# A three-layer transformer kernel on one core: TensorE multiplies constants into the next accumulator before late operands

## What is computed

```
for i in range(DEPTH):                       # DEPTH = 2
    h = rms_norm(x, norm_mix[i]) * (1.0 + sc1) + sh1
    y = mla_mixer(h, ...) if i % 2 == 0 else gdn_mixer(h, ...)
    x = x + g1 * y
    h = rms_norm(x, norm_ffn[i]) * (1.0 + sc2) + sh2
    y = swiglu_ffn(h, ...) if i % 2 == 0 else moe_ffn(h, ...)
    x = x + g2 * y
x = rms_norm(x, final_norm)
x = x + rms_norm_2(merged @ w_out[l], norm_mix_post[l])   # merged: the four gated branches
f = (silu(h @ ffn_w_gate[l]) * (h @ ffn_w_up[l])) @ ffn_w_down[l]
x = x + rms_norm_2(f, norm_ffn_post[l])
```

## Time and profile before

| | |
|---|---|
| median of three runs | 3055.1 us (3048.0 to 3055.36) |
| the profiled execution | 3062.7 us, its span 3061.4 us |
| TensorE busy | 2843.2 us, 93% of the span |
| VectorE busy | 1717.6 us, 56% |
| ScalarE busy | 1235.7 us, 40% |
| GpSimd busy | 248.7 us, 8% |
| mean granted TensorE clock | 0.965 |
| DMA, mean over the span | 127 GB/s |

### The profile page before, as it was taken

How to read it: one execution, slowest core, us unless ns; L and a number is a source line. 1 busy time by engine, 2 the same in 40 slices (tenths; PEclk the granted TensorE clock), 3 DMA queues, 4 the chain that set the end, 5 groups by cost and what they waited for, 6 DMA issues and landing times. The chain is left out here.

```text
span 3061.4 us, 36282 instructions
## 1 busy us (share of the span) xinstructions
PE 2843.2 (93%) x14489; PEld 2326.9 (76%) x14489; DVE 1717.6 (56%) x2889; ACT 1235.7 (40%) x2128; POOL 248.7 (8%) x224
## 2 busy tenths in 40 slices
PE   5988899999997989989999997999999999899998
PEld 4766687877886879778877775788788766678886
DVE  6666455444873857444468886543425386654344
ACT  2455432223433343333467775432223345432222
POOL 0000000000002543010000001112100002200000
PEclk8889999999999999989999999999999999999999
DMA  5222234332222111064579995211231203412321
GB/s 221 76 109 102 83 144 172 137 128 93 96 110 90 56 42 56 1 222 140 186 269 367 342 362 208 76 66 42 101 113 46 83 31 129 150 69 81 116 83 66
DMA packets 72096, 387.66 MB, mean 127 GB/s; under 512 B 8234, under 2 KB 9934, under 8 KB 36174
## 3 DMA queue, kind: packets, MB, share of 16 engines
q1 hardware_dynamic: 58512, 349.20, 31.4%
q10 hardware_dynamic: 10382, 26.07, 2.4%
q0 software_dynamic: 3024, 9.98, 0.9%
HBM read 368.43 MB, written 22.03 MB: 128 GB/s over the span
## 5 line engine op out<-in xcount | busy, mean ns | idle before, releaser
L343 DVE TENSOR_TENSOR wlo<-stage,whi 128x1024 fp32r<-128x1024 f32 (+3 forms) x504 | 531.5, 1095 | 356.2 <-ACT whi L355 354.8
L355 ACT ACTIVATE whi<-stage 128x1024 fp32r<-128x1024 f32 (+3 forms) x504 | 440.4, 922 | 230.8 <-PE ps L639 195.8
L639 PE MATMUL ps<-bxhi,whi 128*128 128x512 f32 x480 | 200.9, 418 | 17.1 <-DVE bxlo L343 8.4
L639 PE MATMUL ps<-whi,mxhi 128*128 128x512 f32 (+1 forms) x528 | 204.2, 387 | 9.9 <-DVE wlo L343 7.8
L639 PE MATMUL ps<-whi,mxlo 128*128 128x512 f32 (+1 forms) x528 | 197.8, 375 | 0.0
L639 PE MATMUL ps<-wlo,mxhi 128*128 128x512 f32 (+1 forms) x528 | 197.5, 374 | 0.0
L639 PE MATMUL ps<-bxhi,wlo 128*128 128x512 f32 x480 | 190.4, 397 | 0.0
L639 PE MATMUL ps<-bxlo,whi 128*128 128x512 f32 x480 | 189.9, 396 | 0.0
L343 DVE TENSOR_TENSOR wlo<-more,whi 128x1024 fp32r<-128x1024 f32 (+1 forms) x126 | 142.2, 1171 | 44.3 <-ACT whi L355 43.1
L351 DVE SCALAR_TENSOR_TENSOR part<-stage,small,part 128x256 f32<-128x256 f32 x273 | 157.9, 579 | 9.7
L639 PE MATMUL ps<-gwide 128*128 128x128 f32 x1088 | 135.8, 285 | 13.4 <-POOL gwide L343 11.5
(11 more groups left out here) (591 smaller groups left out, 6311.6 us busy)
## 6 DMA issues: line engine op xcount, KB each, us to landing
stage<-in_gu SPq DMA_DIRECT2D x92, 1024.0 KB, 5.5
stage<-in_ada SPq DMA_DIRECT2D x40, 1024.0 KB, 5.1
more<-in_gu SPq DMA_DIRECT2D x40, 1024.0 KB, 7.0
stage<-in_dn SPq DMA_DIRECT2D x26, 768.0 KB, 4.5
stage<-in_dn SPq DMA_DIRECT2D x19, 1024.0 KB, 7.1
stage<-in_gin SPq DMA_DIRECT2D x16, 1024.0 KB, 4.9
stage<-in_gt SPq DMA_DIRECT2D x16, 1024.0 KB, 5.0
more<-in_dn SPq DMA_DIRECT2D x13, 1024.0 KB, 6.7
```

The costliest lines, as they stand in the source:

```text
L343: return e.do.tensor_tensor(out, x, y, op)
L355: return e.do.activation(out, x, f, **kw)
L639: return self.p.do.matmul(out, lhsT, rhs, start=start, stop=stop, skip_group_check=True)
```

## The change

A new helper `pe_busy(ps, n)` issues n matmul calls of the block of ones by the first 512 columns of the constants, into the accumulator bank `ps` that the next real operation will overwrite. It stands behind the wait for the bank and ahead of the wait for the operands. Where a wait named operand and bank together, it is cut in two. By the diff there are fourteen places in the order of TensorE: wo 6, xs2 3, gu0 7, xs3 4, gin 7, gq of head 0 4, tt of heads 0, 1 and 4 with 7, 4 and 6, came 0, 1 and 2 with 6, 7 and 2, rw 16, gu2 9. This is 88 calls in one execution. (The part behind the branch is written once for each side of it, and one side runs.)

```diff
+    def pe_busy(self, ps, n):
+        for _ in range(n):
+            self.mm(ps[:, :], self.c("ones"), self.cst_all[:, 0:512])
...
                 if q == 0:
                     p.wait_ge(*vacant)
+                    if step == 0 and first == ids[0:lead]:
+                        self.pe_busy(ps, busy)
                 p.wait_ge(wt(kk), *ok(q))
...
-        self.p.wait_ge(mark, *vacant)
+        self.p.wait_ge(*vacant)
+        self.pe_busy(ps, busy)
+        self.p.wait_ge(mark)
...
-        for _ in self.pe_gemm("wo", "wo", range(4), L.X, lambda q: [V(("ot", "l", q))]):
+        for _ in self.pe_gemm("wo", "wo", range(4), L.X, lambda q: [V(("ot", "l", q))], busy=6):
...
-                for b, _ in enumerate(self.pe_gemm(k, k, ids, L.X, self.normed(L.n.key), lead=2)):
+                for b, _ in enumerate(self.pe_gemm(k, k, ids, L.X, self.normed(L.n.key), lead=2, busy=0 if e or len(ids) == 1 else 9 if layer else 7)):
...
-        self.pe_total("xs2", self.sq, self.V(("wo", "t", 6)), more=self.last_square)
+        self.pe_total("xs2", self.sq, self.V(("wo", "t", 6)), more=self.last_square, busy=3)
...
-        self.pe_total("xs3", self.sq, self.V(("f0", "t", 6)), more=self.last_square)
-        for k, _ in enumerate(self.pe_gemm("gin", "gin", range(16), L.X, self.normed("n3"), lead=2)):
+        self.pe_total("xs3", self.sq, self.V(("f0", "t", 6)), more=self.last_square, busy=4)
+        for k, _ in enumerate(self.pe_gemm("gin", "gin", range(16), L.X, self.normed("n3"), lead=2, busy=7)):
...
-                    self.pe_total(("gq", h), A1, A(("gq", h)))
+                    self.pe_total(("gq", h), A1, A(("gq", h)), busy=0 if h else 4)
...
-                    p.wait_ge(G(("tt", h)), *vac)
+                    p.wait_ge(*vac)
+                    self.pe_busy(b, {0: 7, 1: 4, 4: 6}.get(h, 0))
+                    p.wait_ge(G(("tt", h)))
...
-        p.wait_ge(V(("pick", n)), *vacant)
+        p.wait_ge(*vacant)
+        self.pe_busy(ps, (6, 7, 2, 0)[n])
+        p.wait_ge(V(("pick", n)))
...
-        for _ in self.pe_gemm("rw", "rw", range(4), L.X, L.ok, lead=2):
+        for _ in self.pe_gemm("rw", "rw", range(4), L.X, L.ok, lead=2, busy=16):
```

More of the change, by code:

```diff
@@ L582, in halved, with pe_gemm @@
         return hi, lo, lambda kk: self.V(("lo", i, int(kk >= (kc + 1) // 2)))
-    def pe_gemm(self, key, name, ids, X, ok, at=(None, None), lead=1):
+    def pe_busy(self, ps, n):
+        for _ in range(n):
+            self.mm(ps[:, :], self.c("ones"), self.cst_all[:, 0:512])
+    def pe_gemm(self, key, name, ids, X, ok, at=(None, None), lead=1, busy=0):
         p = self.p
@@ L725, in act_rstd, with pe_total @@
         act(a, dst, dst, ACT.Exp, scale=-0.5, **kw).then_inc(*A.up(event))
-    def pe_total(self, use, src, mark, ones=None, more=None):
+    def pe_total(self, use, src, mark, ones=None, more=None, busy=0):
         ps, vacant = self.take(use)
         ones = self.c("ones") if ones is None else ones
-        self.p.wait_ge(mark, *vacant)
+        self.p.wait_ge(*vacant)
+        self.pe_busy(ps, busy)
+        self.p.wait_ge(mark)
         z = self.mm(ps[:, :], ones, src, True, more is None)
```

## The result

The changed kernel took 3074.8 us (3073.3 to 3076.9, four runs) against 3053.2 us (3048.0 to 3055.4, four runs) for the kernel before: a ratio of 1.0073, with a 95% interval of 1.0057 to 1.0090. That is 22.3 us more (17 to 28), so slower by over 0.3%, as forecast; the forecast was +13.7 us on the median.

What follows compares the result with a forecast made beforehand. TensorE, busy 2843 of 3061 us, was taken to bound the kernel. Lateness less clock given back summed over the places to +13.7 us, 3068.8 us on the median of 3055.1; range 3052 to 3079 for 8 in 10.

Steps and rivals of the forecast that it cites:

- Rival 1: All places: fillers fit their room at 0.43 us a call, clock gives back 15.8 us, 3039 us; chance 0.08.
- Rival 3: All places: fillers don't hold the clock, 31 us of lateness paid without return, 3086 us; chance 0.07.
- Wo: At wo: filler 5.2 us in 3.76 of room, late 1.4, clock gives back 2.9; net -1.5 us.
- Route: At came 0, 1, 2: late 4 to 6 us, back 2.9; net +1.0 to +3.2, taken as +3.1 us.
- Rw: At rw: filler 13.8 us in 8.58 of room, late 5.2, back 2.3; net +2.9 us.
- Gu2: At gu2: filler 7.7 us in 5.16 of room, late 2.6, back 2.1; net +0.5 us.
- xs2 and gu0: First SwiGLU's sum and product: late 0.7 and 2.1 more, clock gives back 1.6; net +1.2 us.
- xs3 and gin: The next pair: late 1.8 and 2.1, clock gives back about 1.7; net +2.2 us.
- gq: Head 0's sums of squares: four fillers, clock back sooner than before; +2.3 us, bounds 0.7 and 4.1.
- tt of heads 0 and 1: Transposes of these heads: late 1.9 with 0.5 back, and no low clock; net +1.4 and +1.1 us.
- behind them up to 1280: tt of head 4: late 1.8 us, clock gives back 1.3; net +0.5 us.
- the two unknown prices: Uncertain costs at gq (0.7 to 4.1 us) and came (1.0 to 6), making the total +10 to +18.

Runs made afterwards that it cites:

- e8_rw_double: The changed kernel with 32 filler calls ahead of rw instead of 16: 3088.4 us, ratio 1.0118 to the kernel before.
- e6_came_only: The changed kernel with only the routing's fillers (came 6/7/2), all other counts 0: 3054.5 us, ratio 1.0012 to the kernel before.
- e5_gdn_only: The changed kernel with only the delta-net fillers (gq 4, tt 7/4/6), all other counts 0: 3064.2 us, ratio 1.0039 to the kernel before.

## Why the prediction was right in sign and short in size

**Right.** TensorE bounds the kernel, so a delay is paid in full: +22 for the whole, +13.5 for 13.7 us of fillers added (e8_rw_double). A call costs 0.86 us (13.90 us for 32 records). The waits are of length zero in front of the real operations, and the clock is 1.00 behind wo, gu0, gin, rw and gu2. Its mean rose from 0.965 to 0.974, where 0.98 was expected. The fillers of came 1 stand behind the branch; two of them ran at half clock in two of the three profiles that have them, none in e6_came_only. The parts add up: 6.1 (dense) + 11.9 (delta-net) + 3.7 (route) = 21.7, and the whole is 22.3 by its ratio. Rival 1 failed at its price. Fillers of that price are the half-width ones: they made the kernel faster, as it says, but by 7.6 us (4.9 to 10.4) and not by its 15.8. It had counted 2.9 us at the first expert product, where TensorE idles in the branch whatever the fillers cost. The Trainium skill, "TensorE: Matmul & The Clock Gate", section Back-to-back issue gap, has 216 ns for 512 columns, by which sixteen calls would have taken 3.5 us, an estimate. The trace doesn't agree for plain fp32: they took 13.90 us here. Rival 3 failed at the earlier trace rows's stretches, which are all at full clock but for the expert products.

**The terms.** Take the mean of the profiles that have a place's fillers less the mean of those that have none there (before, with 0, among them; the fitted and half-width kernels left out where they have other fillers). So each term has a second measure. Wo, gu0 and gin together: the F rows sum to +0.8, the others to -1.3, so +2.1, where the terms have -1.5 + 1.2 + 2.2 = +1.9. Route: 2.9 less -0.2, +3.1, where the term is +3.1; but the three profiles with these fillers give 0.61, 3.93 and 4.03, so that it meets so closely is luck. Rw: 2.88 less -0.2, +3.1, for +2.9. Gu2: +0.5 for +0.5. These stand. Within the first sum wo is off: its gain was read as 2.9 us of clock given back, from the one profile of before, and five other profiles show wo without fillers, four of them with the stage 1.1 to 1.4 us shorter than there. The gain of wo is 0.6 us on the mean and not 1.5. The first SwiGLU's places (xs2 and gu0) are off the other way, +0.7 and not +1.2, as is the next pair (xs3 and gin), +2.0 for +2.2. That the three sum to what was forecast is partly luck too.

**The step that failed: the rounds of the delta net.** By the same measure gq costs 4.5 us (2.61, 2.96, 5.58, 5.61, 5.67; nothing without), where I took +2.3, and tt of heads 0 and 1 3.2 (4.09 or 4.10 beside gq's fillers, 2.46 without them), where I took 2.5; behind them up to 1280 another 1.2 for 0.5. That is 8.9 for 5.3, and in time 11.9 (7.9 to 16.2). Two steps were wrong. The clock was to come back while gq's fillers ran, only sooner than before: in three of five profiles it didn't, the fillers took 6.6 us, and the stage came out 5.6 us later, over the 4.1 us that I had as the upper end. And I took what the clock gives back as won once the sums had run faster. In this chain TensorE waits again right behind them, and the fillers make that wait longer. The first wait behind gq's sums is 2.34 us in all five kernels with the change's fillers at gq, and 1.05 us before; the wait behind tt's round is 2.35 or 2.36 us in all five with the change's fillers at tt, and 1.22 us before. Behind the longer waits the clock fell again, in three of five profiles behind the first and in four of five behind the second; behind the shorter ones of before it had not. In e5_gdn_only 1.3 us did come back up to the end of the first wait (6.00 us from the first sum, for 7.33), and the next sixteen matmuls lost 1.4 us again (3.27 us for 1.88). A filler that holds the clock over one gap of a chain that is full of gaps buys little: the low stretch comes at the next one.

With these the sum is 2.1 + 8.9 + 3.1 + 3.1 + 0.5 = 17.7 us, against 22.3 (17.4 to 27.5) measured. Left open is what the other 4.6 us are, if they are anything; and most of what the traces don't show lies with tt, whose +8.2 in time is 5 us above the 3.1 of its one profile, which lies below the interval (4.3 to 12.2). Only profiles of several executions of it could tell.

**The range** held, 3052 to 3079, and the forecast's own part of it, 3060 to 3078, did too. But +22 lies above the +10 to +18 that the two unknown prices could make. The margins for the clock's low stretches and for the spread of the runs took it in, and not the terms.

## What to carry to other kernels

Filling TensorE's waits pays where a long dense stretch follows, and only up to the length of the wait: read the price of a filler from start to start of its records (here 0.86 us a call, not 0.43) and round the count down, since up to 1.5 us of idle time behind the fillers cost no clock here and every microsecond of excess in front of a dense stretch was paid in full. Seven fitted places gave 0.28% (0.12 to 0.44), the whole fitted set 0.34% (0.21 to 0.48), and the same places overfilled lost 0.73%. Put none behind a branch like this one, where the branch and not the data is what is late, and don't count on a gain in a chain that waits every few microseconds: overfilled it lost 11.9 us, and whether fitted fillers win anything there isn't settled. And take a stage's baseline from several profiles: the one profile of before had 7 us of bad luck ahead of the first changed place, and 1.1 to 1.4 us at that place against four of five others.

## What I had not expected of the hardware

**At the branch TensorE is held longer than its data takes.** It stood in the branch for 3.46 us, and for 3.31 to 3.81 us in the other twelve profiles. The first matmul behind it, a filler or came 1 itself, began only afterwards, with 2.56 to 4.55 us of idle time before it, in every kernel. The operand of came 1 is the first of DVE's three `pick` behind the branch's flag, and in the kernel before it was written by 1312.76 (the line below), 1.6 us before the branch ended at 1314.36:

```profile
1312.07 0.69 DVE L343 TENSOR_TENSOR pick<-count,msmall 128x512 f32<-128x512 f32 x1
```

**The clock's low stretches fall differently in each execution.** The 20 runs of before beside e5_gdn_only went from 3043.7 us at a mean clock of 0.973 to 3062.6 at 0.965. The same gap, 2.36 and 2.35 us long, was followed by eight matmuls in 1.82 us in one kernel and in 1.16 us in another. Fillers make their own stages repeat, to 0.03 us at wo, but not the kernel: the four executions of the changed kernel lie within 3.6 us, and the four of e8_rw_double, which has the same fillers and more, within 12.0. The first 322 us, where none stands, differ by 15 us between the profiles.
